# A chunked recurrence with unnormalised queries and keys, results by token rows, and decay sums loaded from memory

## The reference, cut to what matters

```
qc = l2norm(qc) * DK**-0.5 ; kc = l2norm(kc)        # per head, over 128 channels, then repeated for 2 value heads
g = cumsum(log_a) ; kb = k * beta
m = (k @ kb.T) * exp(g_t - g_s) (strictly lower) ; a_qk = (q @ kb.T) * exp(g_t - g_s) (lower)
u, w = solve(I + m, [v, k * exp(g)])
o = (q * exp(g)) @ S + a_qk @ (u - w @ S)
S = exp(g_last) * S + (kb * exp(g_last - g)).T @ (u - w @ S)
y_c = rmsnorm(o) * gdn_norm_w * silu(z)             # per head, over 128 channels
```

## Time and profile before

| | |
|---|---|
| median of 3 runs | 2838.76 us |
| span of the profiled execution | 2836.0 us |
| its own time | not listed apart; the median lies 2.8 us above the span |
| stages in the span | norm 0 to 82, project 82 to 1637, recur 1638 to 2289, merge to the end |
| TensorE matmul, busy | 2729.1 us, 96% |
| VectorE, busy | 1843.0 us, 65% |
| ScalarE, busy | 1240.6 us, 44% |
| GpSimd, busy | 1471.9 us, 52% |
| granted TensorE clock, mean | 0.984 of full speed |

### The profile page before, as it was taken

The page is one execution under the profiler, slowest core; times in us unless marked ns, Lnnn a source line. Parts: engine busy times, 40 slices in busy tenths (PEclk is TensorE's granted clock), DMA queues, the critical chain, the costliest instruction groups (busy, mean ns, idle before and its releaser), DMA issues. The chain is left out here.

```text
span 2836.0 us, 39388 instructions
## 1 busy us (share of the span) xinstructions
PE 2729.1 (96%) x14135; PEld 2284.9 (81%) x14135; DVE 1843.0 (65%) x2902; ACT 1240.6 (44%) x2154; POOL 1471.9 (52%) x1135
## 2 busy tenths in 40 slices
PE   6899999999998999999999979999999989999999
PEld 5788888888886888888888868888888867888887
DVE  6677777773338788888732258888888855445453
ACT  6443444444444434343444335565556533222221
POOL 0545555454445455555544556667776534453541
PEclk9999999999999999999999979999999989999999
DMA  5333333333453333333334356555556557455552
GB/s 173 99 110 97 112 91 103 108 107 91 119 158 115 122 97 106 88 112 108 97 101 119 97 145 154 146 134 132 134 152 155 135 173 239 157 183 169 177 174 76
DMA packets 536937, 366.05 MB, mean 129 GB/s; under 512 B 65462, under 2 KB 469032, under 8 KB 536744
## 3 DMA queue, kind: packets, MB, share of 16 engines
q1 hardware_dynamic: 536744, 363.52, 45.0%
HBM read 251.27 MB, written 112.20 MB: 128 GB/s over the span
## 5 line engine op out<-in xcount | busy, mean ns | idle before, releaser
L767 POOL TENSOR_TENSOR w_low<-w_raw,w_high 128x512 fp32r<-128x512 f32 x480 | 686.1, 1435 | 635.7 <-ACT w_high L845 635.7
L799 PE MATMUL p_x<-h_high,w_high 128*128 128x512 f32 x1280 | 501.1, 391 | 16.8 <-POOL w_low L767 7.5
L799 PE MATMUL p_x<-h_low,w_high 128*128 128x512 f32 x1280 | 500.5, 391 | 0.0
L799 PE MATMUL p_x<-h_high,w_low 128*128 128x512 f32 x1280 | 500.5, 391 | 0.0
L845 ACT ACTIVATE w_high<-w_raw 128x512 fp32r<-128x512 f32 x480 | 297.1, 626 | 246.3 <-PE p_z L799 139.9
L799 PEld LDWEIGHTS p_x<-h_high,w_high 128*128 128x128 f32 x1280 | 241.7, 189 | 69.3 <-POOL w_low L767 7.6
L799 PEld LDWEIGHTS p_x<-h_low,w_high 128*128 128x128 f32 x1280 | 241.7, 189 | 50.5
L799 PEld LDWEIGHTS p_x<-h_high,w_low 128*128 128x128 f32 x1280 | 241.7, 189 | 50.2
L799 PE MATMUL p_z<-h_high,w_low 128*128 128x512 f32 x640 | 249.0, 389 | 0.0
L799 PE MATMUL p_z<-h_high,w_high 128*128 128x512 f32 x640 | 249.0, 389 | 0.0
L799 PE MATMUL p_z<-h_low,w_high 128*128 128x512 f32 x640 | 249.0, 389 | 0.0
(11 more groups left out here) (299 smaller groups left out, 6082.2 us busy)
## 6 DMA issues: line engine op xcount, KB each, us to landing
w_raw<-in_w_in_dram SPq DMA_DIRECT2D x160, 512.0 KB, 5.2
branch_scratch<-ring SPq DMA_DIRECT2D x176, 256.0 KB, 5.2
gate_scratch<-ring SPq DMA_DIRECT2D x96, 256.0 KB, 6.0
ring<-gate_scratch SPq DMA_DIRECT2D x96, 256.0 KB, 4.0
hin<-branch_scratch SPq DMA_DIRECT2D x16, 1280.0 KB, 11.4
zin<-branch_scratch SPq DMA_DIRECT2D x16, 1024.0 KB, 7.0
m_wo_raw_lead<-in_w_out_c_dram SPq DMA_DIRECT2D x43, 256.0 KB, 3.0
xin<-in_x_dram SPq DMA_DIRECT2D x16, 512.0 KB, 4.0
```

What stands on the lines that cost most here:

```text
L767: nc.gpsimd.tensor_tensor(wl[:, j, :, :], place(p, j), wh[:, j, :, :].bitcast(F32), ALU.subtract).then_inc(low, 1)
L799: x = nc.tensor.matmul(to[:], w[:, j, k, :], h[:, j, k, :], start=(opens and k == 0 and a == 0), stop=(k == HK - 1 and a == 2), skip_group ...
```

## The change

Queries and keys stay as they are loaded. TensorE turns them (`turn_keys`), ScalarE copies the turned keys and squares both from PSUM (`square_keys`), VectorE sums over the free dimension (`key_lengths`), and ScalarE makes of 4 numbers per token a reciprocal square, and a length (`lengths`). The reciprocal squares go into beta and the key decays on GpSimd (`scales`), the lengths into the copy of the values (`copy_v`, now 4 copies of 128x256), and the squares of the queries into epsilon of the output norm. The keys get a second buffer, `kin_odd`.

The outputs of C are laid out by token rows (operands of L1700 and L1701 exchanged). Their lengths are sums over the free dimension (`result_lengths`), `rstd_c` works on 4 numbers per token and scales 4 heads of 128x128 in copies, and `turn_o` turns them back in the next window, after `level_z(w, 4)`; `result_c` there is one operation per half instead of two.

The sums of log decays of all windows are made once, in `project`, by 4 products and 2 transposes (pairs 8 and 10), copied by ScalarE and written to memory. `recur` loads the columns once, and per window two blocks of rows spread over all partitions (`load_centred`, `load_start`, 512 KB each). GpSimd subtracts the column from the row in 8 operations of 128x128 (`exponents`). `pair_kq` moves from VectorE to GpSimd. The causal mask is filled early in `project`, and the squares of the first window at its end are gone.

The order moves with it: `load_z` waits for `y_c` of the window before last, which `result_c` now gives in the middle of a window; `products_ks` comes behind `level_w(w, 4)`; `turn_hv` comes at the end of the window before. The diff at its core:

```diff
+                    for i, which in enumerate((causal[:], after, keep["ones"][:], centred)):
+                        x = nc.tensor.matmul(sums_bank[:, i, :], which, ab[:, :, 0:dm.vh], start=True, stop=True)
...
+                    for i, at in enumerate((0, 3)):
+                        x = nc.tensor.transpose(rows_bank[:, i, :], kept_sums[:, at, :], keep["ident"][:])
...
+                    if p == 8:
+                        decay_sums_of()
+                    if p == 10:
+                        decay_rows_of()
...
+                        sp.dma_start(front["decay_rows"].rearrange("i r n -> r i n"), kept_rows).then_inc(decays_out, 16)
+                        sp.dma_start(front["decay_sums"], t3_flat[:, 0:4 * P]).then_inc(decays_out, 16)
...
+                        tt(centred, causal[:], spread(causal[:, P // 2 - 1:P // 2], P), ALU.subtract).then_inc(sum_masks, 1)
+                        tt(after, keep["ones"][:], causal[:], ALU.subtract).then_inc(sum_masks, 1)
...
+                    wait(sp, w - 2, "m_ks", 2)
+                    wait(sp, w - 2, "qg_ready", 1)
+                    sp.dma_start(kin[w % 2][:], s_dram[of_c:of_c + NK, :, cut(w)].rearrange("t p n -> p t n")).then_inc(k_in, 16)
...
+                def load_centred(v):
+                    wait(sp, v - 1, "diff_ready", 8)
+                    sp.dma_start(rows_centred[:].rearrange("p h n -> p (h n)"), bass.AP(rows.tensor, (win + v) * V * P, [[0, P], [1, V * P]])
...
+                def load_z(w):
+                    wait(sp, w - 2, "y_c", 2)
...
+                sp.dma_start(col[:].rearrange("p i w c -> p (i w c)"), front["decay_sums"]).then_inc(col_in, 16)
+                load_centred(0)
+                load_z(0)
+                load_h(0)
+                load_start(0)
...
                 for w in range(win):
                     if w >= 1 and w + 1 < win:
-                        load(w + 1)
+                        load_h(w + 1)
                     if w + 2 < win:
-                        load_k(w + 2)
+                        load_centred(w + 2)
                     if w > 0:
-                        store(w - 1)
+                        store_h(w - 1)
+                    if w >= 1 and w + 1 < win:
+                        load_z(w + 1)
+                    if w > 0:
+                        store_c(w - 1)
                     if w == win - 1:
                         lead_in()
                     if w + 1 < win:
                         blocks_out(w + 1)
+                        load_start(w + 1)
+                    if w + 2 < win:
+                        load_k(w + 2)
+                    if w + 1 < win:
                         inverses_back(w + 1)
...
+                    for h in range(V):
+                        nc.gpsimd.tensor_scalar(dec[:, h, :], rows_centred[:, h, :], col[:, 3, v, h:h + 1], 0.0, ALU.subtract, ALU.min
...
+                    tt(halves(nb[:, v % 2, :]), halves(neg_b[:, v, :]), inverse, ALU.mult).then_inc(sems["scaled"], 1)
+                    tt(halves(decay_k[:, v % 2, :]), halves(col[:, 1, v, :]), inverse, ALU.mult).then_inc(sems["scaled"], 1)
...
+                    nc.gpsimd.tensor_scalar(eps_q[:, v % 2, :], lens[:, v % 2, 0:Q], EPS * P * P, EPS * EPS * P * P, ALU.mult, ALU.add
...
                     v = w + 1
                     if w > 0:
+                        pair_kq(w)
+                        if v < win:
+                            scales(v)
+                            betas(v)
                         differences(w, 1)
-                    decayed_queries(w)
-                    differences(w, 2)
                     if v < win:
                         weighted_decays(v)
+                    differences(w, 2)
                     decayed_keys(w)
                     differences(w, 3)
                     differences(w, 4)
-                    if v + 1 < win:
-                        log_decays(v + 1)
+                    decayed_queries(w)
                     differences(w, 5)
                     differences(w, 6)
                     differences(w, 7)
                     if v + 1 < win:
-                        betas(v + 1)
-                        squares(v + 1)
+                        exponents(v + 1)
                     state_operands(w)
                     if v < win:
                         differences(v, 0)
...
+                    if v > 0:
+                        pe.wait_ge(k_in, 16 * v)
                     wait(pe, v - 2, "s_done", 8)
...
-                    for g in range(2):
-                        mm(M[g][:], keep["ones"][:], sq[:, g, :], start=True, stop=True).then_inc(sems["m_ssq"], 1)
...
+                    for q in range(Q):
+                        x = turn(M[0][:, q, :], keys(v, q), ident)
+                    x.then_inc(sems["m_turned"], 1)
+                    for q in range(Q):
+                        x = turn(M[1][:, q, :], queries(v, q), ident)
+                    x.then_inc(sems["m_turned"], 1)
...
+                def turn_o(w, g):
+                    wait(pe, w, "yt_ready", 4 * g + 4)
+                    if w + 1 < win:
+                        wait(pe, w + 1, "vt_ready", 2 * g + 2)
+                    for h in range(4):
+                        x = turn(M[2 + g][:, h, :], sqc[:, 4 * g + h, :], ident)
+                    x.then_inc(sems["m_ot"], 1)
...
                 for w in range(win):
                     v = w + 1
                     if w > 0:
                         turn_v(w)
-                        products_ks(w)
                     level_w(w, 4)
                     if w > 0:
-                        turn_k(w)
-                        turn_hv(w)
-                    if 0 < w < win - 1:
-                        decays_between(v)
+                        products_ks(w)
                     level_z(w, 4)
+                    if w > 0:
+                        turn_o(w - 1, 0)
+                        turn_o(w - 1, 1)
                     if 0 < w < win - 1:
                         products_kq(v)
                     if w > 0:
                         scores(w, 0)
-                    if 0 < w < win - 1:
-                        decays_from_start(v)
                     level_w(w, 5)
                     if w > 0:
                         scores(w, 1)
...
                     turn_hk(w)
                     products_ds(w, 0)
-                    norm_c(w, 0)
                     products_ho(w)
-                    norm_c(w, 1)
                     products_hds(w)
+                    if v < win:
+                        turn_hv(v)
                     if v + 1 < win:
-                        norms(v + 1)
+                        turn_keys(v + 1)
                     norm_h(w)
+                for g in range(2):
+                    turn_o(win - 1, g)
             @block.scalar
             def _(act):
...
+                    wait(act, v - 1, "lens_ready", 1)
+                    wait(act, v, "m_turned", 1)
+                    fn(kt[:, v % 2, :, :], M[0][:], ACT.Copy).then_inc(sems["kt_ready"], 1)
+                    fn(sq[:, Q:NK, :], M[0][:], ACT.Square).then_inc(sems["sq_ready"], 1)
+                    wait(act, v, "m_turned", 2)
+                    fn(sq[:, 0:Q, :], M[1][:], ACT.Square).then_inc(sems["sq_ready"], 1)
...
+                    fn(ln_k[:, v % 2, :], lens[:, v % 2, Q:NK], ACT.Ln, bias=eps).then_inc(sems["ln_ready"], 1)
+                    wait(act, v, "ln_ready", 1)
+                    fn(inv_k[:, v % 2, :], ln_k[:, v % 2, :], ACT.Exp, scale=-1.0).then_inc(sems["ln_ready"], 1)
+                    fn(len_k[:, v % 2, :], ln_k[:, v % 2, :], ACT.Exp, scale=0.5).then_inc(sems["ln_ready"], 1)
...
                 def copy_v(w):
+                    wait(act, w, "ln_ready", 3)
                     for g in range(2):
                         wait(act, w, "m_vt", g + 1)
...
+                        for j in range(2):
+                            q = 2 * g + j
+                            fn(vt[:, 2 * q:2 * q + 2, :], M[2 + g][:, 2 * j:2 * j + 2, :], ACT.Copy, scale=len_k[:, w % 2, q:q + 1]
+                               ).then_inc(sems["vt_ready"], 1)
...
-                    fn(G[g][:], G[g][:], ACT.Exp, scale=NEG_HALF).then_inc(sems["rnc_ready"], 1)
+                    fn(rstd_o[:, cut], var_o[:, cut], ACT.Exp, scale=NEG_HALF).then_inc(sems["rnc_ready"], 1)
+                    wait(act, w, "rnc_ready", 2 * g + 2)
+                    for h in range(4 * g, 4 * g + 4):
+                        fn(sqc[:, h, :], M[2 + g][:, h % 4, :], ACT.Copy, scale=rstd_o[:, h:h + 1]).then_inc(sems["yt_ready"], 1)
...
+                def key_lengths(v):
+                    wait(dve, v, "sq_ready", 2)
+                    wait(dve, v - 2, "scaled", 3)
+                    nc.vector.tensor_reduce(lens[:, v % 2, :], sq, mybir.AxisListType.X, ALU.add).then_inc(sems["lens_ready"], 1)
...
+                def result_lengths(w, g):
...
```

(18 more changed lines are left out.)

387 lines of the change are left out of this document (183 added, 204 removed).

## The result

The change makes the kernel slower: 2913.03 us (median of 4 runs, 2903.49 to 2914.91) against 2837.10 us of the kernel before in the same session, a ratio of 1.0266 (95% interval 1.0246 to 1.0286). The profiled execution has a span of 2909.9 us against 2836.0.

What follows compares the result with a forecast made beforehand. VectorE's order, then memory beside ScalarE, was taken to bound each window. Per window 0.0 + 3.0 + 0.2 - 0.25 = +2.9, x14 = +41; with +1, +5, +1 around, +48: span 2884, time 2887 us, range 2822 to 2930.

Steps and rivals of the forecast that it cites:

- rival C: Clock falls in the recurrence: two to six falls in 14 windows add 20 to 60 us, 2906 to 2946; chance 0.2.
- the likeliest case: The forecast itself, `ak` held back on SyncE: 2887 us, spanning 2862 to 2906; chance 0.5.
- a clock under 0.95 in the windows: Sign named in advance that the forecast is wrong and the clock falls.
- The hold: SyncE: `ak` queues behind zin's load and C's store; VectorE waits 3.4 us for X instead of 0.35, +3.0 per window.
- TensorE's 5 us less, credited with nothing: Per window 7.1 us of work gone, 2.1 new, net -5.0; no gain credited, since VectorE then memory set the path.
- The last stretch: Last substituted row to next residual: 12.35 us before, 12.1 taken, -0.25 per window; bounds 10.9 and 13.5.
- VectorE up to the substitution: From residual to substitution: the keys go, -1.28 us, `result_c` comes, +1.5; net +0.2 per window.
- `key_lengths`: VectorE, in front of the residual: 1.2 us taken; bounds twice 0.74 and twice 1.22, the upper called likelier.
- GpSimd: Per window eight exponents at 0.45 us, 3.6; stays near 26.7 of 37.9 us, costed at nothing, under 1 us of cover.
- Around the windows: Outside the windows: `project` +1 us, the start +5 (0 to +8), the end +1.
- Rivals A and B: A: `ak` not held back, 2828 to 2846, chance 0.2. B: window follows TensorE, 2774 to 2782, chance 0.1.

Runs made afterwards that it cites:

- the fourth run: Changed kernel with only the load of zin moved behind `ak` and X, the store of branch C still in front; 2908.06 us, ratio 1.0239.
- the first run: Changed kernel with the load of zin and the store of branch C issued behind `ak` and X; 2879.58 us, ratio 1.0164.
- twelfth run: The eleventh run with the products of the keys with S again in front of the products of T with `ak`; 2849.07 us, ratio 1.0041.
- the eighth run: Changed kernel with late transfers, gap filled, decayed keys later, and window 0's scales and weighted decays ahead of the first differences; 2832.84 us, ratio 0.9997.
- the fifth run: The first run with products repeated in TensorE's gaps (two heads of level 2 scores, first half of level 6), 1.1 us; 2836.98 us, ratio 1.0008.
- the eleventh: The eighth run with decayed keys one more level later and three heads of level 1 scores done twice; 2823.38 us, ratio 0.9963.
- run 43: Not a run's number: the text reads "the first run 43 us faster", where 43 us is a time and the run is the first run.

## Why the prediction was right or wrong

2887 us was forecast, 2913 measured; that lies in the range (2822 to 2930), but in the case of rival C (2906 to 2946, chance 0.2), laid over the forecast's own mechanism. Its own range ended at 2906 (its terms, 4.3 us per window and 10 around them, make 2909), so the likeliest case as I had put it did not hold. Of the signs I had named, those of the hold came (a wait of 2.9 us for X, `ak` landed some 9 us after `zin`'s issue), and so did the one against it, a clock under 0.95 in the windows; the period is 42.3 and not 40.7.

*The hold* was right in kind and size: +3.0 us per window forecast, X at r + 18.8 with `ak` 9.7 us after `zin`'s issue; measured X at 1787.48 - 1769.01 = r + 18.5, issue of X 9.05 us after `zin`'s, and +3.2 us from residual to X on average. What it had wrong is that the wait costs VectorE's time alone: put into the kernel before, the same hold cost 5.9 us a window, 2.3 of them in the fall of the clock behind it. That a queue serves in order was taken from two rows; the fourth run shows a limit, since 0.5 MB in front cost 0.6 us and not 1.8.

*TensorE's 5 us less, credited with nothing*: this is the step that failed, together with the wait priced without the clock. It is not nothing but a loss: the stretch from X to the last row, costed at no change, is 1.9 us longer. Of the 26 us between forecast and measurement this makes +27; the last stretch gave 5 back, and around the windows there are 3.5 more than forecast. Either cause keeps the clock falling without the other: with the gap filled and X held the time is 2915, with X freed and the gap left it is 2880. The 5 us themselves are not found: by the records TensorE is busy for 34.0 us in a window of the first run without a fall, against 37.1 before, 3.1 less; which of my terms was too large I did not trace. The profile before had the sign: a clock of 1.00 in all windows with TensorE at 98%, and 0.50 for 24 us after the one thin stretch at the start. I took that for a rare case and gave two to six falls of 24 us that cost about 10 each; it is one fall of 6.5 to 14 us in each of fourteen windows, at some 2 us each. That the total of rival C (20 to 60 us over the forecast) came out is luck: too few falls at too high a price. The Trainium skill, "TensorE: Matmul & The Clock Gate", section "HAM oscillation — how this bites in real kernels", says that waits between groups of products bring the clock down again and again. The trace agrees in that, once a window in the changed kernel; the section's case is waits for loads, while the gaps here are waits of 0.63 to 0.77 us for VectorE.

*The last stretch*: -0.25 forecast; 12.4 us before and 11.8 now on average, -0.6. ScalarE's chain does bind it (twelfth run), but has less in it than I had.

*VectorE up to the substitution*, +0.2: with the hold away it is 15.9 against 15.2 (first run). The 0.7 are not the exchanged operations but `kql`, 1.11 us before by the median and 2.05 in the first run, beside the decayed keys. *`key_lengths`*: the row is 1.22 us, as taken from L1029; the bounds that I wrote down, twice 0.74 and twice 1.22, did not even hold the value I took. The Trainium skill, "VectorE: DVE Perf Modes", section "Rules for kernel authors", calls the operation the slowest; the trace does not show it slower than a plain operation on as many elements.

*GpSimd*: an exponent takes 0.72 us, not 0.45 (L1506 was not its kind), so eight take 5.7 and not 3.6; the cover held all the same.

*Around the windows*: `project` ended 1.0 us earlier, not 1 later. The first residual came 6.5 us late, near the 5 forecast, for another reason: `ak` landed in 3.2 us there, but was issued 7.4 us later, among other things since GpSimd waited for `hin` with the scales of window 0 queued behind (in the eighth run, with the scales in front, it is issued at 1657.2, not at 1658.2 to 1660.2). What the rest of the 6.5 us is made of was not traced. From the last residual to the end there are 6.3 us more instead of 1, with a fall of the clock in the last window among them. In sum, from the two traces: start +6.5, first window -2.3, fourteen periods +63.4, the rest +6.3, together the 73.9 us between the spans.

*Rivals A and B* fell: `ak` is held, and TensorE's queue does not set the window (in the fifth run it is busy for 34.8 us instead of 37.1, and the period is 37.5 instead of 37.8).

Open: in some windows of the late runs T came 1 to 2 us late (stretches of 12.5 us and more), which I have not traced, and why the same gaps let the clock fall in one window and not in the next. One hint: in the changed kernel each of the four falls at r + 10 comes one window after a fall that began at r + 14.7 to 15.6. And the size of a gap alone does not decide: waits of 1.0 to 1.2 us for W came with a fall in every window of the twelfth run and in two of fourteen of the eleventh, and 1.38 us for T at 1909.82 of the fifth with none.

## What to carry to other kernels

Where TensorE is at 98% and its clock at 1.00, work taken from it is not free: look where it stood, and whether the place is thin without it; here 1.1 us of repeated products in the gap gave 3 us a window back, once X was not held. Before a load gets a new wait, look at what the queue holds behind it, and for whom; a load of 1 MB and a store of 0.5 MB in front of an urgent write of 0.5 MB cost 3 us a window in waiting, and behind it nothing; with the store alone in front there was no wait either. And after each step that makes another engine faster, read the clock again before judging it: the same step cost some 20 us with the gap open and was part of the best version with it closed.

## What was not expected of the hardware

- A VectorE operation of 128x512 (`kql`) took 0.68 us at its shortest. Where it began beside a GpSimd operation of 128x1024 (1.9 us) it ended 0.55 us behind that one's end, both times looked at: 1.11 us in the kernel before, where it began near the other's end (1880.04), and 2.12 in the first run, where it began 0.3 us behind the other's start (1811.53). It seems to wait for the other's end.
- The fall of the clock is not the same in windows that look equal: after 3 us with 1.7 us of work in them it fell or stayed. Moving one GpSimd operation, with TensorE's work the same, changed 9 windows with a fall into 13.
- 1.1 us of repeated products per window made the kernel of the first run 43 us faster.
- A load that spreads 512 KB over all partitions from 4 KB of memory landed 4.2 us after its issue at best, no sooner than a load of 512 KB of different data.
